# A two-block transformer kernel on one core: the second block run twice on 256 tokens, the first time while expert rows are still gathered

## The chip, the cores and the metric

The kernel runs on one core of a Trainium2 chip. The metric is the time of one execution on the device, in microseconds.

## The reference, cut to what matters

The input is 512 tokens of width 1024. The first block (adaptive norm, windowed attention, a short convolution, and a product-key expert layer) is followed by a second block: a matrix-LSTM layer, cross-attention to 256 memory rows, an MLP of width 4096, then a pooling mixer, cross-attention and an MLP again. All are float32. The part of the expert layer that the change is about, and the parts of the second block that tie tokens together:

```python
        ue = jnp.take(u_tab, idx, axis=0)          # 128 rows of 1024 for each token
        ve = jnp.take(v_tab, idx, axis=0)
        act = gelu(jnp.einsum('thkd,td->thk', ue, t))
        return jnp.einsum('thk,thkd->td', (g * act), ve)
...
def second_block(x, mem, ...):
    for i in range(DEPTH_2):                       # 2 layers
        y = mlstm_mixer(...) if i == 0 else pool_mixer(...)
        x = layer_norm(ALPHA * x + y, ...)
        x = layer_norm(ALPHA * x + memory_cross_attn(...), ...)
        x = layer_norm(ALPHA * x + sq_relu_mlp(...), ...)
```

In the second block a token depends on itself and on earlier tokens only (the LSTM's decay sums, a causal convolution over 4 tokens, means over the last 2 to 16 tokens). So tokens 0 to 255 can pass through all of it without tokens 256 to 511.

## The kernel before, in words

Features lie on partitions, tokens along the free axis. A weight tile (128 outputs x 1024 inputs, 512 KB) is streamed from HBM into a ring of four by SyncE. ScalarE rounds it to `whi` (`upper`), VectorE forms the rest `wlo` (`lower`), and TensorE forms `whi*x`, `whi*xlo`, `wlo*x` for 8 blocks of inputs: 24 matmuls of 512 columns for one tile (`feature_product`). The second block has 195 of the 277 tiles. Products go round four PSUM banks (`RING`); bank 4 to 7 serve sums, scores and transposes. All engines run code in the order in which it is written and meet at semaphores.

The expert layer has 512 *picks*: pick p is one expert row for each of 128 tokens (p // 128 is the group of tokens). GpSimd gathers u and v of a pick together, 128 rows of 8 KB (1.05 MB), into one of 8 slots (`gather`, line 400). VectorE multiplies u by the tokens and adds up (`expert_dot`, line 1743). ScalarE applies GELU, multiplies by the gate, and scales an identity matrix by it (`expert_weight`, lines 1145, 1149, 1154). TensorE multiplies this diagonal by v, two float32 matmuls of 512 columns, into banks 4 and 5 (`expert_sum`, line 676). After each 128 picks the sums are turned and added to `xres` (`turn_peer`, `add_peer`). VectorE chooses experts 32 picks at a time, between dots (`top_keys`, `top_pairs`, `pick_experts`; a *unit*). Between picks 288 and 415, 16 weight tiles of the memory's keys and values are worked on.

Only when pick 511 is added does the second block begin: `norm 3`, the LSTM's 17 input tiles (`lstm`), its heads (`core`, 8 tiles), its output (`lout`, 8), then for each layer cross-attention (`xq`, `xo`, 8 tiles each) and MLP (64 tiles), with the pooling mixer (2 tiles, part of it on GpSimd) between the layers. After every one a layer norm over features needs all eight products, so TensorE waits for a chain over ScalarE and VectorE.

Of the kernel before, what the change touches and what calls it, by code (L numbers as in the profile page):

```python
# [6 lines left out]
ALU = mybir.AluOpType  # L7
ACT = mybir.ActivationFunctionType
AX = mybir.AxisListType
F32 = mybir.dt.float32  # L10
# [19 lines left out]
SLOTS = 8  # L30
# [4 lines left out]
MEM_AT, MEM_EVERY = 288, 8  # L35
FF = 4096
WINDOWS = (2, 4, 8, 16)
MIX_ORDER = (1, 0, 3, 2, 5, 4, 7, 6)
# [16 lines left out]
for _name, _n in (("ident", P), ("ones", P), ("perm", P), ("iota", P), ("utri", P), ("band", 3 * P), ("cos", T),  # L55
                  ("sin", T), ("cnt", 4 * 16)):
    _CONST[_name] = (_at, _n)
    _at += _n
# [3 lines left out]
def plan():  # L62
# [37 lines left out]
    section("lstm", [1] * 17)  # L100
    section("core", [1, 1, -2] * 4)
    section("lout", [1] * 8)
    for layer in range(2):
        if layer:
            section("pool", [4] * 2)
        section(f"xq{layer}", [1] * 4 + ([-2] + [1] * 2) * 2 + [-2, -2])
        section(f"xo{layer}", [1] * 8)
        section(f"mlp{layer}", [1] * 4 + ([1] * 4 + [2] * 4) * 7 + [2] * 4)
# [5 lines left out]

SEMAPHORES = (
    "tile_done", "early_done", "bank_free0", "bank_free1", "bank_free2", "bank_free3", "w_loaded0", "w_loaded1",
    "w_loaded2", "w_loaded3", "w_split", "consts_in", "vecs_in", "ctx_in", "conds_in", "mod_dot", "mod_in0",
    "mod_in1", "mod_in2", "mod_in3", "x_in", "mod_used", "norm_out", "stored", 
# [4 lines left out]
    "diagonal", "pick_used", "peer_summed", "peer_copied", "peer_turned", "experts_in0", "experts_in1", "experts_in2",  # L123
    "experts_in3", "experts_in4", "experts_in5", "experts_in6", "experts_in7", "ident_ready",
    "mem_split", "split3", "rows_ready", "decay_turned", "floor_read", "max_spread", "lstm_weighted",
    "qk_ready", "lstm_scores", "head_rms_read", "decay_copied", "lstm_den", "decay_arg", "floor_spread",
    "head_squares", "head_rms", "lstm_split", "pool_split", "x_scores_read", "x_scores", "x_probs", "x_turned_copied",
    "x_turned", "split4", "split5", "split6", "split7", "split8", "hidden_split", "squared", "inverse_ready",
# [3 lines left out]
    "pool_added", "x_shift", "x_exp", "mlp_start", "ppad_zero", "pool_step", "odd_split", "act_step", "dve_step",  # L132
# [3 lines left out]
def build(nc, a, out):  # L136
    ctx = ExitStack()
    with ctx:
# [31 lines left out]
        slots_all = placed("slots", [P, SLOTS, 2 * D], split_at)  # L170
        identr = placed("identr", [P, P], arena_at + 4 * 8192, F32R)[:, :]
        mem_hi = placed("mem_hi", [P, KB, CT], arena_at, F32R)
        mem_lo = placed("mem_lo", [P, KB, CT], arena_at + 4 * 2048, F32R)
# [48 lines left out]
        cand = flat_acc[:, 1024:1536]  # L222
        look = flat_acc[:, 1536:2048]
        tokens = work[:, :, :].rearrange("p k t -> p (k t)").rearrange("p (t d) -> p t d", t=TT)
        dot_out = ar(12288, 1024)
        diag = flat_acc[:, 512:768].rearrange("p (a n) -> p a n", a=2)

        def peer_tokens(t):
            return tiles_of(8192 if t < 2 else 4096, 2, T)
# [1977 lines left out]
```

## Time and profile before

| | us |
|---|---|
| median of 3 runs | 3341.86 (3335.34 to 3342.62) |
| the profiled execution | 3341.29 |
| its span | 3339.2 |
| mean granted TensorE clock | 0.943 |

The span is the time from the first instruction to the last; the rest of the profiled execution's time, 2.1 us, lies around it. A page of the profile gives for each engine the busy time and its share, then the same in 40 slices of the span. A busy TensorE is not one at its peak: its matmuls overlap in the records, and the distance from one start to the next is what one costs in a row.

### The profile page before, as it was taken

Reading aid. Unit: us, or ns where it says so; the run is one execution under the profiler, and the core shown is the slowest. Engines: PE = TensorE matmul, PEld = TensorE weight load, DVE = VectorE, ACT = ScalarE, POOL = GpSimd, SP = SyncE. Lnnn points to the kernel's source line nnn. Section 1 sums busy time; section 2 is a strip of 40 time slices with the busy share of each in tenths; the row PEclk is TensorE's granted clock in tenths of the full one; section 3 lists DMA queues with packets and bytes.
Section 4 is the critical chain, followed back from the end, with each engine's and each line's share of the span. In section 5 each row is a group of like instructions: output and inputs, shape, how many; then the busy total and the mean of one; then the engine's idle time right before and its main releaser. Section 6 shows DMA issues by size and latency. Waiting matters only on the chain. (4 is left out here: it accounts for less than half of the span.)

```text
span 3339.2 us, 32780 instructions
## 1 busy us (share of the span) xinstructions
PE 2908.7 (87%) x10628; PEld 1918.4 (57%) x10628; DVE 2063.9 (62%) x4038; ACT 1193.9 (36%) x2627; POOL 581.1 (17%) x545
## 2 busy tenths in 40 slices
PE   6999899877778777888878789989899986989998
PEld 6777777523333323444433257767788864778886
DVE  6785454566666667667766463665644467564445
ACT  3346323343333333444433344332322223332222
POOL 0000000344444444443434300000000011000000
PEclk9999799999999998999999989999999987999998
DMA  6531122899999999999999922111222220122221
GB/s 243 194 114 57 42 91 70 320 421 419 419 410 417 419 414 406 421 416 417 410 410 421 422 79 69 45 59 61 76 95 94 94 76 19 57 82 95 91 98 51
DMA packets 126110, 719.24 MB, mean 215 GB/s; under 512 B 13200, under 2 KB 16400, under 8 KB 60176
## 3 DMA queue, kind: packets, MB, share of 16 engines
q0 software_dynamic: 73728, 536.90, 39.0%
q1 hardware_dynamic: 46560, 161.18, 14.4%
q10 hardware_dynamic: 5680, 19.40, 1.6%
q8 instruction: 72, 1.18, 0.1%
q14 instruction: 70, 0.57, 0.0%
HBM read 715.33 MB, written 2.10 MB: 215 GB/s over the span
## 5 line engine op out<-in xcount | busy, mean ns | idle before, releaser
L676 PE MATMUL psum<-slots,acc 128*128 128x512 f32 x2048 | 1007.3, 638 | 256.0 <-ACT acc L1154 255.4
L676 PEld LDWEIGHTS psum<-slots,acc 128*128 128x128 f32 x2048 | 390.8, 201 | 851.6 <-ACT acc L1154 445.5
L1743 DVE SCALAR_TENSOR_TENSOR arena<-slots,work 128x1024 f32<-128x1024 f32 x512 | 627.9, 1226 | 401.3 <-DMA slots<-in_experts,consts 385.2
L400 POOL DMA_INDIRECT slots<-in_experts,consts x512 | 553.4, 1081 | 1362.1 <-PE psum L676 713.6
L431 PE MATMUL psum<-xhi,whi 128*128 128x512 f32 x1104 | 445.7, 404 | 3.7 <-DVE wlo L1376 3.7
L432 PE MATMUL psum<-xlo,whi 128*128 128x512 f32 x1104 | 436.8, 396 | 0.0
L433 PE MATMUL psum<-xhi,wlo 128*128 128x512 f32 x1104 | 436.7, 396 | 0.0
L1376 DVE TENSOR_TENSOR wlo<-w,whi 128x1024 fp32r<-128x1024 f32 x277 | 336.8, 1220 | 153.0 <-ACT whi L954 152.0
L954 ACT ACTIVATE whi<-w 128x1024 fp32r<-128x1024 f32 x277 | 291.1, 1052 | 287.3 <-PE psum L433 287.3
L431 PE MATMUL psum<-yhi,whi 128*128 128x512 f32 (+1 forms) x736 | 296.6, 403 | 34.1 <-POOL ylo L418 21.1
L1145 ACT ACTIVATE consts<-consts 128x1 f32<-128x1 f32 x512 | 101.7, 199 | 574.5 <-DVE arena L1743 573.3
L432 PE MATMUL psum<-ylo,whi 128*128 128x512 f32 (+1 forms) x736 | 293.7, 399 | 0.0
L433 PE MATMUL psum<-yhi,wlo 128*128 128x512 f32 (+1 forms) x736 | 293.5, 399 | 0.0
L1154 ACT ACTIVATE acc<-consts 128x128 f32<-128x128 f32 x512 | 205.5, 401 | 174.4 <-PE psum L676 159.4
L431 PEld LDWEIGHTS psum<-xhi,whi 128*128 128x128 f32 x1104 | 207.8, 188 | 59.1 <-issue 10.6
L433 PEld LDWEIGHTS psum<-xhi,wlo 128*128 128x128 f32 x1104 | 207.5, 188 | 50.7
L432 PEld LDWEIGHTS psum<-xlo,whi 128*128 128x128 f32 x1104 | 207.7, 188 | 49.8 <-issue 1.6
L431 PEld LDWEIGHTS psum<-yhi,whi 128*128 128x128 f32 x736 | 141.4, 192 | 73.5 <-issue 25.5
L432 PEld LDWEIGHTS psum<-ylo,whi 128*128 128x128 f32 x736 | 141.8, 193 | 33.8 <-issue 0.2
L433 PEld LDWEIGHTS psum<-yhi,wlo 128*128 128x128 f32 x736 | 141.4, 192 | 33.7
L1149 ACT ACTIVATE consts<-consts 128x1 f32<-128x1 f32 x512 | 150.8, 295 | 17.6
L2056 DVE TENSOR_TENSOR acc<-acc,psum 128x512 f32<-128x512 f32 x112 | 77.0, 688 | 123.1 <-PE psum L433 123.1
(266 smaller groups left out, 3036.5 us busy)
## 6 DMA issues: line engine op xcount, KB each, us to landing
w<-in_stream SPq DMA_DIRECT2D x277, 512.0 KB, 3.4
arena<-in_wmod SPq DMA_DIRECT2D x4, 2048.0 KB, 17.8
arena<-in_wmod ACTq DMA_DIRECT2D x8, 1024.0 KB, 6.0
acc<-in_wmod ACTq DMA_DIRECT2D x8, 1024.0 KB, 7.9
slots<-in_experts,consts POOLq DMA_INDIRECT x512, 13.3
xres<-in_xT SPq DMA_DIRECT2D x1, 2048.0 KB, 15.2
outT<-xres SPq DMA_DIRECT2D x8, 256.0 KB, 2.0
consts<-in_consts SPq DMA_DIRECT2D x1, 1056.0 KB, 5.0
```

The costliest lines, as they stand in the source:

```text
L400: pool.indirect_dma_start(out=slots[p % SLOTS], out_offset=None, in_=a["experts"], in_offset=bass.IndirectOffsetOnAxis(ap=indices[:, p:p + ...
L431: pe.matmul(dst, hi, xh(k), start=(j == 0), stop=False)
L432: pe.matmul(dst, hi, xl(k), start=False, stop=False)
L433: mm = pe.matmul(dst, lo, xh(k), start=False, stop=(j == len(ks) - 1))
L676: mm = pe.matmul(bank(4 + half), diag[:, p % 2, :], v[:, half * T:(half + 1) * T], start=(c == 0), stop=(c == PICKS - 1))
L954: act.activation(whi[:, s, :, :].rearrange("p k n -> p (k n)"), w32[:, s, :], ACT.Copy)\
L1145: act.activation(gelus[:, c:c + 1], inner[:, c:c + 1], ACT.Gelu).then_inc(sem("gelu_ready"), 1)
L1149: act.activation(weights[:, c:c + 1], gelus[:, c:c + 1], ACT.Copy, scale=gates[:, p:p + 1])\
L1154: act.activation(diag[:, p % 2, :], ident, ACT.Copy, scale=weights[:, c:c + 1])\
L1376: dve.tensor_tensor(wlo[:, s, :, :].rearrange("p k n -> p (k n)"), w32[:, s, :], whi[:, s, :, :].rearrange("p k n -> p (k n)").bitcast(F32 ...
L1743: dve.scalar_tensor_tensor(dot_out, slots[p % SLOTS][:, 0:D], 1.0, tokens[:, p // PICKS, :], ALU.mult, ALU.mult, accum_out=inner[:, c:c + ...
L2056: free(dve.tensor_tensor(acc[:, k, :], acc[:, k, :], bank(oo % RING), ALU.add), oo)
```

## The change

- The whole second block is written as functions of a half (`half_lstm_in`, `half_lstm_core`, `half_cross`, `half_mlp`, `half_pool`), called for tokens 0 to 255 and then for 256 to 511. So its 195 weight tiles are streamed, rounded and split twice (472 tiles in all, 277 before), each with 24 matmuls of 256 columns. In the MLP's second layer two outputs of a tile share one bank of 512.
- Picks 0 to 255 go as before, but into 6 slots at first, which grow to 10 (`SLOT_OPENS`). A unit's choice follows each 21 picks instead of 32 (`TOP_AT`), with 3, 3 and 4 dots between its parts. The memory's tiles come at picks 96 to 223.
- Picks 256 to 511 are spread over the first half's tiles by a table (`pick_ends`): 1 share for a tile, 2.4 for a tile of `core`, 2.5 to 6 for a norm. That is 10 picks ahead of the first tile, 71 over the first MLP's tiles and 71 over the second's. TensorE's part is `sum_picks`, ScalarE's `weigh_picks`, VectorE's `dot_picks`.
- For these picks u and v are gathered apart, 4 KB rows from two tables, v two picks behind u: 4 places for u, 6 and later 8 for v.
- Two of these picks are added at once by eight matmuls with 64 rows and 64 columns of weights and 512 columns of data (`expert_pair`), into four banks: rows 0 to 63 of v into banks 4 and 5, rows 64 to 127 into 6 and 7. The diagonal is 128 x 64.
- In the first half products have two banks instead of four (`out_banks`), sums and norms banks 2 and 3. The loops over the MLP's groups are written out.
- The pooling mixer is on VectorE alone. The first half's outputs are stored from GpSimd's queue.

```diff
-SLOTS = 8
+EARLY = NPICKS // 2
-MEM_AT, MEM_EVERY = 288, 8
+MEM_AT, MEM_EVERY = 96, 8
+H = T // 2
+HT = H // P
...
+    for half in range(2):
+        section(f"lstm{half}", [1] * 17)
+        section(f"core{half}", [-1 - half, 1, 1, -3] * 4)
+        section(f"lout{half}", [1] * 8)
...
+    first, last = SECTIONS["lstm0"][1], SECTIONS["lstm1"][1]
+    banks = [o % (2 if first <= o < last else RING) for o in range(len(DONE))]
...
+    gaps = {SECTIONS["lout0"][0] + 7: 2.5, SECTIONS["pool0"][0] + 1: 2.5, SECTIONS["mlp0"][0] + 63: 6}
...
+    length = {n: 2.4 if n in core else 1.0 for n in range(first, last)}
+    total = sum(length.values()) + sum(gaps.values())
+    head = EARLY + 10
...
+SLOT_OPENS = {60: 7, 84: 6, 144: 8, 228: 9}
...
+U_ROWS, V_ROWS, V_OPEN, LEAD = 4, 6, 300, 2
...
+LATE_UNITS = 12
+TOP_AT = {u: 2 + 21 * (u - 1) if u < LATE_UNITS else EARLY + 1 + 11 * (u - LATE_UNITS) for u in range(1, UNITS)}
...
-            for p in range(NPICKS):
+            for p in range(EARLY):
                 gather(p)
...
+            for p in range(EARLY, NPICKS + LEAD):
+                if p < NPICKS:
+                    gather_u(p)
+                if p >= EARLY + LEAD:
+                    gather_v(p - LEAD)
...
+            def expert_pair(p):
+
+                t, c = p // PICKS, p % PICKS
+                if c == 1:
+                    pe.wait_ge(sem("peer_added"), 8 * t)
+                for q in (p - 1, p):
+                    row, _, uses = V_USE[q - EARLY]
+                    pe.wait_ge(sem(f"v_in{row}"), 16 * uses)
+                pe.wait_ge(sem("diagonal"), p + 1)
+                for half in range(2):
+                    for q in (p - 1, p):
+                        for r in range(2):
+                            rows = slice(64 * r, 64 * r + 64)
+                            to = 64 * (r ^ (q % 2))
+                            mm = pe.matmul(psum[to:to + 64, 4 + 2 * r + half, :], diag(q)[rows, :],
+                                           v_row(q)[rows, half * T:(half + 1) * T], start=(c == 1),
+                                           stop=(c == PICKS - 1))
+                        if half:
+                            mm.then_inc(sem("pick_used"), 1)
...
+            def sum_picks(n):
+
+                nonlocal summed
+                while summed < picks_by(n, True):
+                    expert_sum(summed)
+                    if summed % PICKS == PICKS - 1:
+                        turn_peer(summed // PICKS)
+                    summed += 1
...
+            def half_linear(n, o, XH=XHH, XL=XLH):
+                linear(n, o, XH, XL, H)
+                sum_picks(n)
...
+            for half in range(2):
+                half_lstm_in(half)
+                half_lstm_core(half)
+                half_cross(half, 0)
+                half_mlp(half, 0)
+                half_pool(half)
+                half_cross(half, 1)
+                half_mlp(half, 1)
```

The order in which TensorE goes over the first MLP's tiles shows the first term: these rows are matmuls (line, output, inputs, columns). Before:

```order
L431 MATMUL psum<-yhi,whi 128x512
L432 MATMUL psum<-ylo,whi 128x512
L433 MATMUL psum<-yhi,wlo 128x512
L431 MATMUL psum<-yhi,whi 128x512
L432 MATMUL psum<-ylo,whi 128x512
```

In the changed kernel, the first half, where one tile ends and the next begins:

```order
L604 MATMUL psum<-xhi_h,whi 128x256
L605 MATMUL psum<-xlo_h,whi 128x256
L606 MATMUL psum<-xhi_h,wlo 128x256
L874 MATMUL psum<-arena,consts 64x512 x8
L604 MATMUL psum<-yhi_h,whi 128x256
L605 MATMUL psum<-ylo_h,whi 128x256
L606 MATMUL psum<-yhi_h,wlo 128x256
```

A matmul has half the columns, and between two tiles of every second pick stand the eight of 64 weights' columns.

VectorE in the second layer of the MLP, where a tile's rest (`wlo`) is formed and the hidden values are squared and split. Before:

```order
L2040 TENSOR_TENSOR work<-work 128x512
L1382 CAST yhi<-work 128x512
L1384 TENSOR_TENSOR ylo<-work,yhi 128x512
L1376 TENSOR_TENSOR wlo<-w,whi 128x1024
L2040 TENSOR_TENSOR work<-work 128x512
```

In the changed kernel, the first half, where outputs are collected and the next group's first hidden tile comes (line 2035 is the dot of one pick):

```order
L1656 TENSOR_TENSOR wlo<-w,whi 128x1024
L2035 SCALAR_TENSOR_TENSOR slots,consts<-slots,work 128x1024
L2401 TENSOR_TENSOR acc<-acc,psum 128x512
L1656 TENSOR_TENSOR wlo<-w,whi 128x1024
L2035 SCALAR_TENSOR_TENSOR slots,consts<-slots,work 128x1024
L2401 TENSOR_TENSOR acc<-acc,psum 128x512
L1656 TENSOR_TENSOR wlo<-w,whi 128x1024
L2035 SCALAR_TENSOR_TENSOR slots,consts<-slots,work 128x1024
L2401 TENSOR_TENSOR acc<-acc,psum 128x512
L1656 TENSOR_TENSOR wlo<-w,whi 128x1024
L2035 SCALAR_TENSOR_TENSOR slots,consts<-slots,work 128x1024 x2
L2394 TENSOR_TENSOR work<-work 128x256
```

The rest of a tile has its 1024 columns as before, the hidden values have 256, and about one dot of a pick stands at each tile.

GpSimd's queue of gathers, with what each waits for. Before:

```order
L400 DMA slots<-in_experts,consts 128x2048 x3
L400 DMA slots<-in_experts,consts 128x2048 [waits pick_used] x24
L400 DMA slots<-in_experts,consts 128x2048 [waits pick_used,picked]
L400 DMA slots<-in_experts,consts 128x2048 [waits pick_used] x31
L400 DMA slots<-in_experts,consts 128x2048 [waits pick_used,picked]
```

In the changed kernel, late in the first half:

```order
L578 DMA arena<-in_expert_v,consts 128x1024 [waits pick_used]
L563 DMA slots<-in_expert_u,consts 128x1024 [waits dotted,picked]
L578 DMA slots<-in_expert_v,consts 128x1024 [waits pick_used]
L563 DMA slots<-in_expert_u,consts 128x1024 [waits dotted]
L578 DMA slots<-in_expert_v,consts 128x1024 [waits pick_used]
```

A pick has two gathers of 1024 columns, where u waits for a dot four picks back, and v for a sum.

## Rows read from the trace of the kernel before

**Rows 1.** The page: busy time of the engines, DMA in 40 slices

```profile
PE 2908.7 (87%) x10628; PEld 1918.4 (57%) x10628; DVE 2063.9 (62%) x4038; ACT 1193.9 (36%) x2627; POOL 581.1 (17%) x545
DMA  6531122899999999999999922111222220122221
```

**Rows 2.** By stretch: us, PE, PEld, DVE, ACT, POOL busy, clock, DMA share, GB/s

```profile
617.00:1930.00 1313.00, 1054.58 (x2486) 444.86 (x2484) 891.12 (x2056) 524.96 (x1679) 549.35 (x508) 0.94 1.01 414
1930.00:1968.00 38.00, 25.30 (x94) 18.86 (x95) 24.96 (x50) 17.90 (x29) 0.00 (x0) 0.78 0.00 1
1968.00:2057.00 89.00, 85.40 (x384) 68.77 (x384) 44.23 (x53) 39.24 (x55) 0.00 (x0) 0.99 0.30 100
2057.00:2161.00 104.00, 103.84 (x426) 72.43 (x426) 69.35 (x109) 36.47 (x52) 0.00 (x0) 0.98 0.10 31
2161.00:2206.00 45.00, 43.70 (x200) 35.03 (x198) 27.59 (x39) 13.60 (x18) 0.00 (x0) 1.00 0.29 87
2221.00:2308.00 87.00, 80.34 (x320) 59.51 (x320) 53.98 (x129) 31.91 (x63) 0.00 (x0) 0.96 0.14 44
2308.00:2353.00 45.00, 44.76 (x192) 35.91 (x192) 19.75 (x27) 11.06 (x14) 0.00 (x0) 1.00 0.23 75
2353.00:2367.00 14.00, 6.64 (x35) 5.97 (x34) 10.29 (x19) 4.58 (x6) 0.00 (x0) 0.70 0.26 91
2367.00:2730.00 363.00, 361.12 (x1536) 289.32 (x1536) 196.25 (x260) 99.04 (x116) 0.00 (x0) 0.99 0.28 90
2730.00:2797.00 67.00, 26.29 (x82) 20.58 (x83) 58.56 (x96) 19.50 (x29) 27.41 (x28) 0.63 0.06 21
3317.00:3339.00 22.00, 6.50 (x33) 6.02 (x32) 13.79 (x25) 7.23 (x10) 0.00 (x0) 0.59 0.25 95
```

**Rows 3.** Timeline of GpSimd: the first gathers

```profile
618.55 0.93 POOL L400 DMA_INDIRECT slots<-in_experts,consts  x1 [29.84 <-PE psum L433]
619.78 0.94 POOL L400 DMA_INDIRECT slots<-in_experts,consts  x1 [0.30 <-issue]
```

**Rows 4.** Waits of the whole span: total us, times, longest

```profile
POOL slots L400 <- PE psum L676: 713.6, 414, 8.7
DVE arena L1743 <- DMA slots<-in_experts,consts: 385.2, 312, 2.4
```

**Rows 5.** Timeline of TensorE, 512 and 256 columns, then a run of sums

```profile
2400.14 0.40 PE L431 MATMUL psum<-xhi,whi 128*128 128x512 f32 x1
2400.38 0.39 PE L432 MATMUL psum<-xlo,whi 128*128 128x512 f32 x1
...
1351.66 0.28 PE L433 MATMUL psum<-mem_hi,wlo 128*128 128x256 f32 x1
1351.78 0.28 PE L431 MATMUL psum<-mem_hi,whi 128*128 128x256 f32 x1
...
1439.82 7.21 PE L676 MATMUL psum<-slots,acc 128*128 128x512 f32 x16
```

**Rows 6.** Groups of VectorE by form, 1960 to 3339 us

```profile
L1376 DVE TENSOR_TENSOR wlo<-w,whi 128x1024 fp32r<-128x1024 f32 x191 | 232.1, 1220 | 71.6 <-ACT whi L954 71.5
L2056 DVE TENSOR_TENSOR acc<-acc,psum 128x512 f32<-128x512 f32 x112 | 77.0, 688 | 123.1 <-PE psum L433 123.1
```

**Rows 7.** Groups of VectorE by form, 700 to 1900 us

```profile
L1743 DVE SCALAR_TENSOR_TENSOR arena<-slots,work 128x1024 f32<-128x1024 f32 x467 | 572.8, 1227 | 365.6 <-DMA slots<-in_experts,consts 350.9 <-issue 3.2
L1743 DVE DVE_READ_ACCUMULATOR arena<-slots,work 128x1 f32 x467 | 38.6, 83 | 0.0
L1384 DVE TENSOR_TENSOR mem_lo<-acc,mem_hi 128x256 fp32r<-128x256 f32 x8 | 3.4, 426 | 0.3
L1382 DVE CAST mem_hi<-acc 128x256 fp32r<-128x256 f32 x8 | 2.3, 289 | 0.0
```

**Rows 8.** A group of ScalarE by form, 700 to 1900 us

```profile
L1145 ACT ACT_TABLE_LOAD x14 | 18.0, 1283 | 0.2
```

**Rows 9.** A group of TensorE by form, whole span

```profile
L589 PE MATMUL psum<-arena 128*64 128x128 f32 x288 | 44.2, 306 | 0.7 <-ACT arena L1063 0.7
```

More of the change, by code:

```diff
@@ L99, in plan @@
     section("memv", [1] * 8)
[L100 to L108, printed above, removed]
+    for half in range(2):
+        section(f"lstm{half}", [1] * 17)
+        section(f"core{half}", [-1 - half, 1, 1, -3] * 4)
+        section(f"lout{half}", [1] * 8)
+        for i in (2 * half, 2 * half + 1):
+            if i % 2:
+                section(f"pool{half}", [4] * 2)
+            section(f"xq{i}", [1] * 4 + ([-1] + [1] * 2) * 2 + [-1, -1])
+            section(f"xo{i}", [1] * 8)
+            section(f"mlp{i}", [1] * 64)
@@ new lines, in pick_ends, with by @@
+def pick_ends():
+    first, last = SECTIONS["lstm0"][0], SECTIONS["lstm1"][0]
+    core = range(SECTIONS["core0"][0], SECTIONS["lout0"][0])
+    gaps = {SECTIONS["lout0"][0] + 7: 2.5, SECTIONS["pool0"][0] + 1: 2.5, SECTIONS["mlp0"][0] + 63: 6}
+    groups = [first]
+    for i in range(2):
+        gaps[SECTIONS[f"xo{i}"][0] + 7] = 2.5
+        groups += [SECTIONS[f"xq{i}"][0], SECTIONS[f"mlp{i}"][0]]
+    length = {n: 2.4 if n in core else 1.0 for n in range(first, last)}
+    total = sum(length.values()) + sum(gaps.values())
+    head = EARLY + 10
+    ends, at = {first - 1: (EARLY, head)}, 0.0
+    def by(at):
+        return head + round((NPICKS - head) * at / total)
+    for n in range(first, last):
+        begin = ends[n - 1][1]
+        at += length[n]
+        end = begin if n in groups else by(at)
+        at += gaps.get(n, 0)
+        ends[n] = (end, by(at) if n in gaps else end)
+    assert ends[last - 1][1] == NPICKS
+    return ends
@@ new lines, with picks_by, slot_uses @@
+PICK_ENDS = pick_ends()
+def picks_by(n, gap=False):
+    return PICK_ENDS[n][gap] if n in PICK_ENDS else EARLY if n < SECTIONS["lstm0"][0] else NPICKS
+SLOT_OPENS = {60: 7, 84: 6, 144: 8, 228: 9}
+SLOT_UNITS = {7: 4, 8: 8, 9: 12}
+def slot_uses():
+    free, slots = [4, 5, 0, 1, 2, 3], []
+    for p in range(EARLY):
+        if p in SLOT_OPENS:
+            free.insert(0, SLOT_OPENS[p])
+        slots.append(free.pop(0))
+        free.append(slots[-1])
+    before, uses, last = [], [], {}
+    for p, slot in enumerate(slots):
+        before.append(last.get(slot))
+        uses.append(slots[:p + 1].count(slot))
+        last[slot] = p
+    return slots, before, uses, last
@@ L1337, in _ @@
[L1337 to L1346 removed]
+                n, o = SECTIONS[f"xo{q}"]
```

1697 lines of the change are left out of this document (958 added, 739 removed).

## The prediction

> **What bounds the kernel now.** I read the page first: TensorE is busy 87% of the span, but the DMA line shows two halves that look unlike each other, full for some 16 slices and at one to two tenths after them [rows 1]. So I cut the span into stretches [rows 2]. From 617 to 1930 us the DMA engines are busy throughout at 414 GB/s, while VectorE is busy for 891 of 1313 us and ScalarE for 525. These are picks 4 to 511: 508 gathers and 16 weight tiles of half a gather's size each, so 1313 / 516 = 2.545 us for a gather and 1.27 us for a tile. VectorE waits for rows in 312 places, 385 us in all; GpSimd's wait for TensorE (714 us) is only the wait for a free slot [rows 4]. This stretch is bound by DMA, and TensorE's work in it (two matmuls a pick) is covered. Then the second block starts, and DMA is nearly idle: an MLP takes 363 us with TensorE busy in 361 of them, `lout` 45 us for 8 tiles, and only the norms, the pooling stretch (67 us, TensorE busy 26) and `core` hang on other engines [rows 2]. So the span now is 617 us up to the gathers that flow, 1313 of DMA, and 1409 mostly of TensorE. The change tries to lay half of the first bound beside half of the second.
>
> **Prices.** TensorE: one matmul of 512 columns starts 0.234 us after the one before it, one of 256 after 0.12 (0.118 over the run that these rows are from) [rows 5]. A tile of 24 costs 5.6 us before and 2.83 now: a half costs half, weights loaded twice or not. A float32 matmul of a pick has 7.21 us for 16, which overlap, so about 0.43 each and 0.86 for a pick [rows 5]. VectorE: a tile's rest has 1.22 us and does not shrink; collecting an MLP output of 512 columns 0.69 [rows 6]; 256 columns 0.43, as a cast 0.29; a dot 1.23 + 0.08 = 1.31 [rows 7]. A unit's choice of experts: (891 - 508 x 1.24 - 20 for 16 rests - 14 for splits and sums) / 15 = 15 to 16 us busy, about 18 with the gaps between dependent instructions [rows 2, 7].
>
> **Part 1, up to pick 255.** Before, picks 0 to 3 are gathered while the slots of the rest wait 29.8 us for the projection, to 618.6 [rows 3]. Now only two slots are free of it, so 254 rows come after: 254 x 2.545 + 16 x 1.27 = 667 us. Six slots instead of eight are less cover. A slot's round is 8 x 2.545 = 20.4 us before and 15.3 with six; a landing, dot, diagonal, sum and new gather need some 9 of it (my sum of those rows). A unit's three parts now have 10 dots between start and end: 31 us for which DMA needs 25.5, and with the peaks VectorE falls up to 11 us behind where six slots cover 6. I take 4 to 5 us for each of the three units before pick 60 and 4 for the rest: +18. Part 1 ends at 618.6 + 667 + 18 = 1303.
>
> **Part 2, the first half with 256 picks.** In the MLP a tile has 71/64 = 1.11 picks. DMA: 1.27 + 1.11 x 2.545 = 4.09 us. VectorE: a hidden tile 1.22 + 0.43 + 0.29 + 0.43 = 2.37, an output tile 1.22 + 0.69 = 1.91, so 2.14 + 1.11 x 1.31 + gaps 0.15 = 3.74. TensorE: 2.83 plus the pick. The trace has no concurrent partial-array matmuls; the nearest row is one of 64 weight columns, 306 ns for 128 columns [rows 9], but it stands alone. Bounds: four quadrants side by side, 2 x 0.43 a pair, 0.43 a pick; all eight one after another, 8 x 0.43 / 2 = 1.72. I take 0.75, near the lower end, as quadrants of other rows and other banks share nothing that the code shows. TensorE then needs 3.66. All three lie within 12% of each other and DMA leads: 64 x 4.09 = 262, +6 for imperfect covering and the slow first tiles: 268 a time, instead of 363 for all tokens.
> Two rules bear on this and pull apart. The Trainium skill, "TensorE: Matmul & The Clock Gate" (Part 3: Packing small matmuls), reports 2.4 to 3.1 times from three or four tiles; by that a pick would have 0.55 to 0.72 us. "TensorEngine Tiling (Array Packing)", Key Properties of the Trainium skill, says that a change of tiling mode drains the engine, which happens twice a pair here. No row of this trace shows either.
>
> The other stages are VectorE's, which carries dots, rests and the half's own chains in program order. Its sum for part 2: 256 dots 335 us, 195 rests 238, 4 units 66, the half's own work about 365 (the instructions of one half at 256 columns), together 1004, gaps 60. By stage: 10 picks, a unit and norm 3: 48; `lstm` 118 (norm output 9, convolution 8 x 4.7, 9 tiles x 2.7, gates 12, two units 36; ScalarE reloads a table for each switch between Silu and GELU, 1.28 us [rows 8], hidden here); `core` 112 (four heads of 23 busy and 5 waited; 104 before); `lout` 36; four norms 14 to 15 each, 58, and the one after the pool 12; `xq` 58 twice, `xo` 36 twice (9 picks each and 8 tiles, 33 by DMA); two MLPs 536; the pooling mixer on VectorE with its norm 50 (8 x 4.1 + 17). Sum 48 + 118 + 112 + 36 + 58 + 12 + 116 + 72 + 536 + 50 = 1158. DMA alone would need 256 x 2.545 + 195 x 1.27 = 899, so it is idle a fifth of this part. Part 2 ends at 2461.
>
> **Part 3, the second half, four banks and no picks.** Halved where TensorE bounds, less where a chain does; the times before are those of [rows 2]: MLP 186 twice (363; VectorE's 2.3 a tile hides under 2.83); `lout` 29; `xo` 23 twice; `xq` 45 twice (87 before, VectorE's softmax and rests now last); norm 3: 15; `lstm` 60 (together 127 before, 1930 to 2057); `core` 78 (104; the same instructions, shorter); four norms 12 (14), with that behind the pool 46; the mixer 40 (67); the end 15 (22). Sum 372 + 29 + 46 + 90 + 15 + 60 + 78 + 46 + 40 + 15 = 791, and the end is at 3252. Plus the 2.1 us around the span: **3255 us** against 3341.3 for the profiled execution, which lies 0.6 us under the median. That is 2.6% less. The gain is small for 652 us of gathering (256 x 2.545) laid beside the half: the half beside it grows from about 791 to 1158, and 195 rests, 238 us of VectorE, come twice in chains of small instructions that did not halve.
> Free: the doubled stream (102 MB, 248 us of DMA in part 3 under 791), the store from GpSimd's queue, and 512 gathers instead of 256 (1.24 us from one issue to the next, 618.55 to 619.78 [rows 3], so 2.5 a pick against 4.09 / 1.11 = 3.7). Were GpSimd slower than that, every MLP tile would follow it.
>
> **Rivals.**
> 1. *Quadrants don't overlap (0.12).* A pick then has 1.72 us and the switches; say 1.9. An MLP tile is bound by TensorE at 2.83 + 1.11 x 1.9 = 4.94, 316 us each instead of 268, +96; some 20 in the other stages: **3370**, slower. It decides from 1.14 us a pick on, where 2.83 + 1.11 x 1.14 passes 4.09. For it: all partial-array matmuls of the trace are single. Against: they share no rows, columns or banks.
> 2. *The engines' orders interlock (0.15).* In the first half products have two banks, so product n + 2 waits until ScalarE or VectorE has read n, and these stand behind a dot (1.31), a rest (1.22) or a table load and a pick's three steps. If reading takes more than the 2.83 us of one product, the difference is lost in each tile; 0.7 us in 195 tiles are 137: **3392**, slower. For it: before, with four banks and no picks, ScalarE and VectorE still wait for each product. Against: both have 3 to 10% left in the MLP and reading comes early after a product.
> 3. *Half-size gathers move less (0.04).* If 12 gathers of 0.5 MB in flight don't fill the engines as 8 of 1 MB did, and a pick costs a third more, 3.4 us, an MLP has 64 x 1.27 + 71 x 3.4 = 323, +110 for two: **3365**, slower. Weight tiles have this size, but never come back to back in the trace; against it, both moves have several in flight. The Trainium skill, "DMA: Bandwidth & Descriptors" (Measured, HBM to SBUF), asks for at least 1 MiB a transfer; no row here shows it.
> 4. *Better covering (0.07).* Twelve places let DMA run ahead in slow stages; part 2 is then VectorE's 1060: **3155**.
>
> **Numbers.** My forecast has 0.62, its own range 3170 to 3330. The measurement can tell about 0.2% (7 us) from no change. Faster: nearly all of mine and rival 4, some of the rest: 0.69; within 7 us 0.04; slower: rivals 1 to 3 but for a sixth, 0.27. The range for all goes from 3140 to 3390, which leaves out the ends of rival 2.
>
> **What would show it.** Pick 255's dot near 1300; then DMA at four fifths; first MLP near 268 us at over 0.9 DMA, TensorE's eight matmuls of a pair in under 2 us; the second half's MLP 186 us each; VectorE over 85% in part 2. I would be wrong most in `lstm` and `core` of the first half, where I added waits by judgement, and by the quadrants.

## The result, and the profile after

The change made the kernel slower by 0.8%: 3367.39 us, median of three runs (3363.34 to 3370.86), against 3341.86 (3335.34 to 3342.62), a ratio of 1.0082 with the interval 1.0055 to 1.0108. I had forecast 3255 us. The direction was wrong.

The page of the kernel after, its line for TensorE and its DMA line, answers to [rows 1]:

```profile
PE 2813.9 (84%) x16524; PEld 2123.3 (63%) x16524; DVE 2377.0 (71%) x5028; ACT 1500.2 (45%) x3177; POOL 882.8 (26%) x781
DMA  6531122799999999686679988479993223551353
```

The full slices of DMA are no longer one block. They end after pick 255, come back twice, in the two MLPs of the first half, and in between stand at six to eight tenths or lower. The stretches answer to [rows 2] (us, busy time of PE, PEld, DVE, ACT and POOL, granted clock, DMA share, GB/s). In order: part 1; norm 3, `lstm`, `core` and `lout` of the first half; `xq` and `xo`; its first MLP; pooling; its second MLP; the first MLP of the second half, each with the norm before it:

```profile
617.00:1318.00 701.00, 562.67 (x1446) 254.40 (x1444) 509.30 (x1268) 284.07 (x883) 290.21 (x257) 0.91 0.98 396
1360.00:1627.00 267.00, 204.22 (x1362) 146.21 (x1361) 216.81 (x520) 158.72 (x326) 119.01 (x105) 0.84 0.74 269
1627.00:1744.00 117.00, 95.88 (x643) 73.08 (x640) 78.29 (x165) 61.51 (x131) 43.23 (x40) 0.88 0.71 250
1744.00:2082.00 338.00, 286.51 (x2213) 219.71 (x2209) 241.36 (x409) 152.73 (x361) 182.01 (x157) 0.93 0.90 343
2082.00:2135.00 53.00, 20.44 (x96) 14.08 (x96) 46.40 (x143) 18.93 (x44) 6.54 (x6) 0.56 0.24 86
2248.00:2556.00 308.00, 276.29 (x2159) 216.16 (x2160) 228.28 (x383) 147.34 (x340) 160.57 (x137) 0.94 0.90 347
2833.00:3031.00 198.00, 186.88 (x1554) 186.01 (x1554) 150.39 (x245) 90.39 (x122) 0.00 (x0) 0.97 0.52 173
```

Beside the forecast: `lstm` to `lout` 267 us (266), `xq` and `xo` with a norm 117 (108), pooling 53 (50), the second half's MLP 198 with its norm (186 + 12). The two MLPs with picks carry the miss: 338 and 308 where 283 had been forecast (268 and a norm). In them no engine and not DMA is full over the whole stretch: TensorE 85% and 90%, VectorE 71% and 74%, DMA 90%. So "which one is the bound" has no answer from this table alone, and the experiments had to give it.

### The profile page after: what moved, and what is told of

It reads as the page before. It is cut to its first block and busy times, and to the rows that moved or that the text cites. A ratio compares the mean times of both kernels' runs of the same rounds, so it can differ in the third digit from the quotient of the medians.

```text
span 3365.6 us, 47654 instructions
## 1 busy us (share of the span) xinstructions
PE 2813.9 (84%) x16524; PEld 2123.3 (63%) x16524; DVE 2377.0 (71%) x5028; ACT 1500.2 (45%) x3177; POOL 882.8 (26%) x781
## 5 line engine op out<-in xcount | busy, mean ns | idle before, releaser
L2035 DVE SCALAR_TENSOR_TENSOR slots<-slots,work 128x1024 f32<-128x1024 f32 x453 | 553.6, 1222 | 131.1 <-DMA slots<-in_experts,consts 107.8
L856 PE MATMUL psum<-slots,acc 128*128 128x512 f32 x788 | 406.3, 658 | 120.1 <-ACT acc L1388 113.8
L544 POOL DMA_INDIRECT slots<-in_experts,consts x197 | 219.4, 1114 | 928.7 <-DVE consts L2007 582.7
L563 POOL DMA_INDIRECT slots<-in_expert_u,consts x256 | 285.9, 1117 | 558.8 <-DVE slots L2035 507.2
L604 PE MATMUL psum<-yhi_h,whi 128*128 128x256 f32 x1312 | 381.1, 290 | 55.7 <-ACT acc L1623 25.8
L604 PE MATMUL psum<-xhi_h,whi 128*128 128x256 f32 x1456 | 420.7, 289 | 3.9 <-DVE wlo L1656 3.9
L605 PE MATMUL psum<-xlo_h,whi 128*128 128x256 f32 x1456 | 410.9, 282 | 0.0
L606 PE MATMUL psum<-xhi_h,wlo 128*128 128x256 f32 x1456 | 410.4, 282 | 0.0
L605 PE MATMUL psum<-ylo_h,whi 128*128 128x256 f32 x1312 | 374.9, 286 | 0.0
L606 PE MATMUL psum<-yhi_h,wlo 128*128 128x256 f32 x1312 | 374.1, 285 | 0.0
L874 PE MATMUL psum<-slots,consts 64*64 64x512 f32 x1080 | 237.7, 712 | 137.9 <-ACT consts L1388 87.3
L604 PEld LDWEIGHTS psum<-yhi_h,whi 128*128 128x128 f32 x1312 | 254.8, 194 | 98.5 <-issue 78.2
L604 PEld LDWEIGHTS psum<-xhi_h,whi 128*128 128x128 f32 x1456 | 278.7, 191 | 44.4 <-issue 36.5
L874 PEld LDWEIGHTS psum<-slots,consts 64*64 64x64 f32 x1080 | 61.6, 150 | 233.3 <-issue 221.6
```

Of the source, the lines that this page charges most:

```text
L544: pool.indirect_dma_start(out=slots[slot], out_offset=None, in_=a["experts"], in_offset=bass.IndirectOffsetOnAxis(ap=indices[:, p:p + 1], ...
L563: pool.indirect_dma_start(out=u_rows[row], out_offset=None, in_=a["expert_u"], in_offset=bass.IndirectOffsetOnAxis(ap=indices[:, p:p + 1], ...
L604: pe.matmul(dst, hi, xh(k), start=(j == 0), stop=False)
L605: pe.matmul(dst, hi, xl(k), start=False, stop=False)
L606: mm = pe.matmul(dst, lo, xh(k), start=False, stop=(j == len(ks) - 1))
L856: mm = pe.matmul(bank(6 + half), diag(p), v[:, half * T:(half + 1) * T], start=(c == 0), stop=(c == PICKS - 1))
```

## The experiments

Runs of one kernel scatter: three of the kernel after lie 7.5 us apart, four of e4 19 and six of h1 22. All of e2, e3, f and g ran once, so a difference of less than some 20 us in their whole time says little; there the stretches within the trace carry the reading. All of batch e shared its runs of before (3339.21 us, seven runs), all of batch f one run (3341.08), all of batch g one (3342.16).

**e1: the kernel before with rows gathered apart.** Only the form of the gather changes: two of 4 KB rows for one of 8 KB rows. The products and their order stay.

```
-                pool.indirect_dma_start(
-                    out=slots[p % SLOTS], out_offset=None, in_=a["experts"],
+                for j, table in enumerate(("expert_u", "expert_v")):
+                    pool.indirect_dma_start(
+                        out=slots[p % SLOTS][:, j * D:(j + 1) * D], out_offset=None, in_=a[table],
...
-                dve.wait_ge(sem(f"experts_in{p % SLOTS}"), 16 * (p // SLOTS + 1))
+                dve.wait_ge(sem(f"experts_in{p % SLOTS}"), 32 * (p // SLOTS + 1))
```

> The kernel before, with u and v of each pick gathered by two DMAs of 4 KB rows instead of one of 8 KB; nothing else differs. In the changed kernel DMA moved only 377 GB/s at a full share in the middle of the first MLP, against 414 before. Theory A (4 KB gathers are slower by themselves): the gathering stretch of 1313 us grows by a tenth, to about 1430, and the time to 3450. Theory B (what slows it is the mix with the stream of weight tiles): 3342, unchanged within 10 us. A third way: GpSimd's 1.24 us for each issue, 2.48 a pick against 2.545, becomes the limit and adds up to 60 us.

Measured: 3505.1 us (four runs), ratio 1.049 (1.0473 to 1.0508), 166 us more over 512 picks. The stretches of this kernel inside its gathering:

```profile
617.00:1300.00 683.00, 487.05 (x972) 191.11 (x970) 411.26 (x986) 229.66 (x759) 489.34 (x474) 0.89 0.97 366
1300.00:2100.00 800.00, 607.09 (x1514) 273.90 (x1515) 480.03 (x1070) 282.28 (x917) 569.63 (x542) 0.87 0.97 367
```

The DMA engines are 97% busy (101% before), but move 366 GB/s instead of 414, 11.6% less. So theory A holds, with more than its 3450 us. GpSimd has 489 of 683 us busy, 72%, so it isn't the full one. A gather in two halves costs about 2.545 + 166 / 512 = 2.87 us. The prediction had charged the late picks 2.545. Whether the shorter rows or the smaller gathers cost this isn't separated: both changed.

**e2: a quarter of u.** The late picks' u rows are gathered over 256 of 1024 columns; a late pick moves 640 KB instead of 1 MB, and its dot stays full length. (Besides the line shown, the table holds only these columns, and the dot's factor is 0.1.)

```
-                    out=u_rows[row], out_offset=None, in_=a["expert_u"],
+                    out=u_rows[row][:, 0:256], out_offset=None, in_=a["expert_u"],
```

> The changed kernel, where a gather of u after pick 255 brings 256 of 1024 columns (the dot still runs over 1024, so its result is another). An MLP tile then moves 0.52 + 1.11 x 0.66 = 1.25 MB instead of 1.69. Theory A (DMA sets the pace of the first half's MLPs): both shrink by 20 to 35 us down to VectorE's 3.7 to 3.9 us a tile, and the whole by 60 to 90 us, near 3290. Theory B (the engines' orders set it, DMA is only busy beside them): less than 20 us in all.

Measured: 3348.5 us, 19 less, at the edge of the scatter and of theory B. The MLPs took 322 and 300 us instead of 338 and 308. Three eighths of a late pick's bytes bought 16 of the 55 us by which the first MLP had missed. From 1780 to 1900 us, inside the first MLP, DMA is no longer full and TensorE is:

```profile
1780.00:1900.00 120.00, 118.86 (x988) 93.66 (x987) 99.00 (x159) 62.05 (x146) 76.83 (x66) 1.00 0.89 306
```

DMA sets some of the pace; TensorE stands close behind it.

**e3: no late picks.** Picks 256 to 511 are neither chosen, gathered, dotted nor summed; two halves and two banks stay. Two of its edits:

```
-            for p in range(EARLY, NPICKS + LEAD):
+            for p in range(0):
...
-                while summed < picks_by(n, True):
+                while False:
```

> The changed kernel without the picks 256 to 511: their choice, gathers, dots, diagonals and sums are left out, everything else stands. It gives the price of the first half alone and so what the picks cost in it. Theory A (halving itself costs little, two banks are enough): the first half takes as long as the second, 800 to 815 us, the whole 2940. Theory B (two banks stall the first half): 850 or more, the whole near 3000.

Measured: 2909.2 us, where theory A had 2940. Four stretches of this kernel, `lstm` to `lout` and the two MLPs of the first half (two banks), then the first MLP of the second half (four banks):

```profile
1326.00:1490.00 164.00, 139.10 (x946) 129.26 (x946) 109.07 (x222) 82.37 (x132) 0.00 (x0) 0.87 0.31 100
1575.00:1777.00 202.00, 189.67 (x1554) 188.25 (x1554) 151.48 (x246) 90.87 (x122) 0.00 (x0) 0.96 0.56 170
1906.00:2108.00 202.00, 189.74 (x1554) 188.23 (x1554) 151.43 (x246) 90.95 (x122) 0.00 (x0) 0.96 0.55 170
2378.00:2576.00 198.00, 186.86 (x1553) 186.00 (x1553) 150.48 (x245) 90.50 (x122) 0.00 (x0) 0.97 0.56 173
```

Without picks two banks cost 4 us an MLP against four. So the half itself is sound, and this run gives a ledger. The start of pick 255's dot and the end of the span are in each trace:

```
                              before    after     e3
pick 255's dot (us)           1262.6    1318.1    1314.5
pick 511's dot                1930.4
end of the span               3339.2    3365.6    2907.4

part 1 longer                 1318.1 - 1262.6                    = + 55.5   (forecast + 40)
gathering of 256 picks gone   1930.4 - 1262.6                    = -667.8
halving the second block      (2907.4-1314.5) - (3339.2-1930.4)  = +184.1   (forecast +173)
256 picks beside a half       (3365.6-1318.1) - (2907.4-1314.5)  = +454.6   (forecast +367)
sum                                                              = + 26.4
```

The 667.8 us hold 16 weight tiles of the memory besides (16 x 1.27 = 20 us), which stand in part 1 of the kernel after and so in its + 55.5. A late pick still costs 454.6 / 256 = 1.78 us of the span, against 2.545 in the gathering, and I had forecast 367 / 256 = 1.43. That one line holds 88 of the 114 us by which the span was missed.

**e4: fewer picks in the MLPs.** The table that shares out the picks gives tiles of the MLPs a weight of 0.85 and the other tiles 1.4 (both 1.0 in the change).

```
-    length = {n: 2.4 if n in core else 1.0 for n in range(first, last)}
+    length = {n: 2.4 if n in core else 1.4 for n in range(first, last)}
+    for i in range(2):
+        at = SECTIONS[f"mlp{i}"][0]
+        for n in range(at, at + 64):
+            length[n] = 0.85
```

> The changed kernel with another table: a tile of an MLP has the share 0.85 and every other tile but those of core 1.4, so that each MLP has some 13 picks fewer. Theory A (in the MLPs DMA bounds with 2.8 us a pick, in the other stages VectorE with 1.3 to 2): 26 picks moved save 25 to 40 us, near 3335. Theory B (the engines' orders bound everywhere alike): 3367 within 10 us.

Measured: 3376.95 us (four runs), ratio to before 1.0129 (1.0101 to 1.0156). The MLPs fell to 307 and 278, but `lstm` to `lout` rose from 267 to 308 and the others by 8 to 14 each. That is theory B: a pick costs about as much elsewhere as in an MLP, and taking picks from the tiles of an MLP isn't the cure.

**f1 to f3: one engine at a time.** f1 takes the quadrants away, f2 shortens the dots, f3 the sums.

```
f1   for r in range(2):
+        if 1 < c < PICKS - 1:
+            if r:
+                mm = pe.matmul(psum[0:64, 4 + 2 * (q % 2) + half, :], diag(q),
+                               v_row(q)[:, half * T:(half + 1) * T], start=False, stop=False)
+            continue
f2
-    dve.scalar_tensor_tensor(u, u, 1.0, tokens[:, p // PICKS, :], ALU.mult, ALU.mult,
+    w = D if p < EARLY else 256
+    dve.scalar_tensor_tensor(u[:, 0:w], u[:, 0:w], 1.0, tokens[:, p // PICKS, 0:w], ALU.mult, ALU.mult,
f3   for r in range(2):
+        if half and 1 < c < PICKS - 1:
+            continue
```

> The changed kernel, but of each pair's eight 64x64 products of the late picks four are issued instead, each over all 128 rows into 64 partitions (all but the first and the last pair of a token tile); the sums are not the reference's. A pick then holds TensorE for 4 records of 0.43 = 1.72 us, where the changed kernel's trace has 82.2 us for 78 picks = 1.05 us in the first MLP. If TensorE paces a stage with picks, each of 240 picks costs 0.67 us more: +52 us in the first MLP (338 to 390) and +160 in all, about 3525 us. If VectorE paces, or the covering costs what it costs by the hand-over from engine to engine, it stays within 40 us of the changed kernel: 3370 to 3410. If quadrants brought nothing in the changed kernel, no change.

Measured: 3487.1 us, 120 more than the kernel after; the first MLP 369 instead of 338, the second 342 instead of 308. The first line below is a pair of picks in the first MLP of the kernel after, with the tile's matmul that follows; the last is one of f1 (TensorE's timeline: start, us, name, operands, records):

```profile
1906.26 0.28 PE L606 MATMUL psum<-yhi_h,wlo 128*128 128x256 f32 x1
1906.47 1.95 PE L874 MATMUL psum<-slots,consts 64*64 64x512 f32 x16
1908.35 0.39 PE L604 MATMUL psum<-yhi_h,whi 128*128 128x256 f32 x1
```

```profile
1885.84 3.65 PE L874 MATMUL psum<-arena,consts 128*64 128x512 f32 x8
```

Eight float32 matmuls leave 16 records, two each, in 1.95 us. From the last matmul of a tile to the first of the next 2.09 us pass, 0.12 of it the tile's own, so a pick takes (2.09 - 0.12) / 2 = 0.98 us. f1's four matmuls, 8 records, take 3.65, 1.83 a pick. So the quadrants do overlap and are worth 0.84 us of TensorE a pick. 248 of the late picks have f1's form (all but the first and the last pair of two token tiles; I had counted 240), and 120 / 248 = 0.48 us of each comes through. That lies between the forecasts for "TensorE paces" (3525) and for "it does not" (3370 to 3410). TensorE is busy in 343 of the 369 us of the first MLP: at f1's price it is nearly the whole bound, at 0.98 it is not.

> The changed kernel with the late picks' dots over 256 of the 1024 columns; the dots are not the reference's. By 1.227 us for 1024 columns a dot falls to some 0.4 us, 0.8 less for each of 256 picks. If VectorE paces: MLP 0's stretch 338 to about 275 us and the whole 3367 to about 3200 (0.65 us a pick and more saved). If TensorE paces (tile 2.9 + 1.2 x 1.05): less than 15 us in all. If the two hand each other over through two banks so that their works add in part: between, 30 to 45 us in MLP 0 and 80 to 130 in all.

Measured: 3371.2 us, no change. VectorE falls from 241 to 181 us in the first MLP, and that takes 337 instead of 338. VectorE does not set the pace there.

> The changed kernel with the late picks' products over the first 512 of the 1024 columns alone, but for the first and the last pair of a token tile; the sums are not the reference's. TensorE's share of a pick falls from 1.05 to about 0.55 us. If TensorE paces: -40 us in MLP 0 (338 to 298) and -115 us in all, 3250. If VectorE paces: less than 15 us. If both add in part: 15 to 25 us in MLP 0, 40 to 80 in all.

Measured: 3361.9 us, 6 less, within the scatter. TensorE's work in the first MLP falls from 287 to 267 us, the stretch from 338 to 334. A pair falls from 1.95 to 1.09 us, which is 34 us for 39 pairs; only 20 come through, and the granted clock of the stretch is 0.87 where it was 0.93. Taken alone, TensorE doesn't set the pace either.

**f4, g1 to g3: several at once.** f4 is e2, f2 and f3 together. g1 is f4 with v gathered over 512 columns besides. g2 has g1's gathers with full dots and products. g3 is f2 and f3 together with full gathers. The one new edit, in g1 and g2:

```
-                    out=v_rows[row], out_offset=None, in_=a["expert_v"],
+                    out=v_rows[row][:, 0:T], out_offset=None, in_=a["expert_v"],
```

> The changed kernel with all three together: u gathered and dotted over 256 columns, sums over 512; neither is the reference's. The kernel without late picks took 2909 us. If three resources share the cost of covering, what is left of the 458 us is ScalarE's part and the issues: by ScalarE's 0.3 + waits for a pick, 2990 to 3080 us. If a fourth thing that none of the three touches paces the picks (the chain dot, weight, diagonal, product from engine to engine, or GpSimd's issues at 2 x 1.34 us a pick, 256 x 2.7 = 690 us against 1240 there are), it stays above 3200 us.

> The kernel with all three light, and v gathered over 512 columns besides (its products read the same 512 columns); a late pick now moves 384 KB instead of 1 MB. It was at 3287 with 640 KB a pick. If the DMA engines still were what bounds it there: 3220 to 3260. If VectorE's and TensorE's order around the picks is: within 12 us of 3287. It also shows what the covering costs at the least: the kernel without late picks took 2909 us.

> The changed kernel with u gathered over 256 columns and v over 512 (384 KB a late pick instead of 1 MB), all dots and products issued in full; neither is the reference's. The quarter u alone gave 3348. If three resources stand close to each other at 4.1 to 4.2 us a tile of the MLP, taking more of one brings nothing more: 3335 to 3350, since TensorE's 268 us of 322 and its gaps stay. If the gathers alone paced: 3290 or less.

> The changed kernel with quarter dots and half sums, the gathers in full; neither is the reference's. Each alone brought -4 and +4 us. If the gathers hold the pace by themselves once the engines are lighter (the DMA engines 0.99 busy in the first MLP, 1.0 MB a pick and 0.5 MB a tile at 366 GB/s = 4.9 us for 1.2 picks and a tile): 3345 to 3367. If VectorE and TensorE paced in turns, so that only both together bring something: 3290 or less.

Measured: f4 3287.0, g1 3273.6, g2 3335.6, g3 3352.6 us. g2 and g3 came out inside the forecasts by which several limits stand close together and the gathers hold g3. For f4 my first case (2990 to 3080, all that is left would be ScalarE's) was far off; its other case, above 3200 with something that none of the three touches, came true, and g1 lies near its "within 12 us of 3287". To see why, here are 120 us of steady running in the first MLP, 1780 to 1900 us, in which it is well under way in each. First the kernel after, then g2, then g3 (a stretch each, columns as above):

```profile
1780.00:1900.00 120.00, 111.52 (x916) 86.92 (x914) 96.60 (x154) 58.91 (x140) 76.57 (x64) 0.99 1.02 397
```

```profile
1780.00:1900.00 120.00, 119.87 (x976) 93.21 (x973) 98.41 (x161) 63.13 (x149) 78.31 (x65) 0.98 0.71 232
```

```profile
1780.00:1900.00 120.00, 103.14 (x814) 87.32 (x814) 71.36 (x150) 58.33 (x136) 67.16 (x64) 0.97 1.02 406
```

And TensorE's groups in the same 120 us, of the kernel after and of g2. L604 leaves eight records a tile; L874 leaves 16 for a pair of picks, (128 + 64 + 64) / 8 = 32 picks here:

```profile
L604 PE MATMUL psum<-xhi_h,whi 128*128 128x256 f32 x124 | 35.6, 287 | 0.0
L604 PE MATMUL psum<-yhi_h,whi 128*128 128x256 f32 x96 | 27.5, 287 | 0.0
L874 PE MATMUL psum<-slots,consts 64*64 64x512 f32 x128 | 23.3, 601 | 5.6 <-issue 5.6
L874 PE MATMUL psum<-acc,consts 64*64 64x512 f32 x64 | 15.5, 602 | 0.0
L874 PE MATMUL psum<-arena,consts 64*64 64x512 f32 x64 | 9.2, 694 | 2.9 <-issue 2.9
```

```profile
L604 PE MATMUL psum<-xhi_h,whi 128*128 128x256 f32 x139 | 40.4, 291 | 0.0
L604 PE MATMUL psum<-yhi_h,whi 128*128 128x256 f32 x96 | 27.5, 286 | 0.0
```

The kernel after does (124 + 96) / 8 = 27.5 tiles, 4.36 us each; DMA is full at 397 GB/s, TensorE has 5.6 + 2.9 = 8.5 us of idle time ("issue": the profile names no releaser; in g2, with light rows, TensorE is idle for 0.13 us, so probably a row of v was not there), so a pick holds it (120 - 8.5 - 27.5 x 2.83) / 32 = 1.05 us. In g2, with light gathers, DMA drops to 0.71 and TensorE is busy for 119.87 of 120 us; it does 29.4 tiles, 4.08 us each. So DMA leads, and TensorE stands 0.28 us a tile behind it: taking DMA away altogether gives 6%. In g3 both engines are light and DMA is at 1.02 and 406 GB/s again; 28.6 tiles. That is why f2 brought nothing, f3 little, and e2 some 19 us: each takes from one of two limits that almost coincide, VectorE's being the third (96.6 of 120). But that isn't all. Even g1, with 384 KB a pick, quarter dots and half sums, is just 2% under the kernel before: its first MLP takes 301 us, and TensorE is busy in 260 of them, DMA 67%:

```profile
1719.00:2020.00 301.00, 259.87 (x1915) 212.95 (x1915) 181.01 (x409) 152.05 (x361) 166.85 (x156) 0.90 0.67 214
```

Sixty-two of its tiles take 256 us, 4.1 each, where TensorE's own work at full clock is some 3.45 (2.83, and 35 pairs of 1.09 over 62 tiles; an estimate). No engine nor DMA is full here. What holds it, the chain from dot to sum or GpSimd's issues (f4's other case), no run isolates.

**h1: the adding of a token tile's sums two dots sooner.** The turn of a token tile falls into the first MLP, at pick 384. Stretches of the kernel after around it, then the three operations on its path (timelines of TensorE and ScalarE), then TensorE's waits from 1935 to 1975 us (total us, times, longest):

```profile
1900.00:1935.00 35.00, 34.56 (x284) 28.00 (x280) 26.03 (x41) 16.64 (x39) 19.56 (x17) 0.99 0.98 369
1935.00:1975.00 40.00, 30.09 (x194) 24.22 (x195) 18.08 (x31) 11.27 (x25) 13.41 (x12) 0.79 0.65 231
1975.00:2010.00 35.00, 31.39 (x261) 25.43 (x261) 25.22 (x42) 16.77 (x39) 20.13 (x18) 1.00 1.00 377
```

```profile
1936.91 1.95 PE L874 MATMUL psum<-slots,consts 64*64 64x512 f32 x16 [2.35 <-issue]
1938.94 2.06 ACT L1398 ACTIVATE slots<-psum 128x512 f32<-128x512 f32 x4 [5.75 <-PE psum L874]
1941.06 6.34 PE L894 MATMUL psum<-consts,slots 128*128 128x64 f32 x32 [2.20 <-ACT slots L1398]
```

```profile
PE psum L874 <- DVE xres L2047: 5.8, 1, 5.8
PE psum L874 <- issue: 2.4, 1, 2.4
PE psum L894 <- ACT slots L1398: 2.2, 1, 2.2
```

The last sum of tile 2, ScalarE's copy, 32 records of turning, VectorE's adding and the first sum of tile 3 stand in series, and while they run rows are not freed: DMA drops to 0.65. VectorE adds only behind the fourth dot of the next tile, and TensorE waits 5.8 us for it.

```
-                    if dotted % PICKS == 3:
+                    if dotted % PICKS == 1:
```

> The changed kernel, with the adding of a finished token tile's sums placed two dots sooner in VectorE's order (after the second dot of the next tile instead of the fourth). In the changed kernel TensorE waits 5.8 us for this adding once in the first MLP (and 5 us before the second tile's first sum), while VectorE has been idle 8 us shortly before. If the stall at the turn of a token tile is an order's fault: 5 to 12 us less, 3355 to 3362, ratio to the kernel before 1.004 to 1.006. If VectorE then waits for the turned sums while dots stand behind it and rows stay ungathered, the loss is the same or more: 3365 to 3375. Neither gets below the kernel before.

Measured: 3354.7 us (six runs, 3343.56 to 3365.58), ratio to before 1.0051 (1.0034 to 1.0067), against 1.0082 for the change. The first MLP fell from 338 to 324 us, and the wait for L2047 is gone from it (its TensorE waits from 1900 to 1975 us):

```profile
PE psum L874 <- issue: 2.6, 1, 2.6
PE psum L894 <- ACT slots L1398: 2.2, 1, 2.2
```

Not all 14 us are the edit's. The trace is of the fastest of the six runs, 11 us under their median. From the tile before the turn to four tiles behind it, 36.5 us (1934.5 to 1971.0) became 28.7: 8 us, the wait and a little more. Another 4 of the 14 lie ahead of the turn, where nothing was changed, and the second half, where nothing was changed either, is 8 us shorter. By the medians h1 gains 13 us, and the two intervals against before overlap. It remains slower than the kernel before; no kernel here that computes the whole is faster than that.

## Why the prediction was wrong, point by point

**Right.** The quadrants overlap (rival 1 had 0.12, and it fell: 0.98 us a pick between two tiles and 1.05 on average over 120 us, below the bound of 1.14). Halving costs what I said, 184 against 173. The second half was forecast at 791 and a norm of 14.5 and took 809. DMA leads in an MLP with picks in steady running, TensorE is close behind and VectorE third, in that order; DMA over the whole of part 2 stood at four fifths, as said. VectorE did not: 75% of part 2 instead of over 85%.

**Right by luck.** `lstm` to `lout` took 267 us for 266, but its three parts missed and made up for each other: `lstm` 108 for 118, `core` 104 for 112, `lout` with the picks behind it 55 for 36.

```profile
1360.00:1468.00 108.00, 81.41 (x575) 60.91 (x574) 93.53 (x251) 72.12 (x141) 42.76 (x37) 0.85 0.70 252
1468.00:1572.00 104.00, 80.31 (x487) 55.35 (x487) 85.02 (x201) 61.96 (x130) 47.57 (x43) 0.84 0.76 270
1572.00:1627.00 55.00, 42.50 (x301) 29.96 (x301) 38.27 (x70) 24.64 (x58) 28.68 (x26) 0.82 0.80 298
```

**Rival 2**, the interlock of products and readers, did not happen in the MLP, and it is the trace of the kernel after that shows it: of TensorE's 51 idle us in the first MLP only the norm's 4.7 stand before products of tiles. The rest, but for 0.6 in the norm, is before picks' sums and the turn, above all these two:

```profile
PE psum L874 <- issue: 23.8, 10, 3.4
PE psum L874 <- ACT consts L1388: 14.5, 3, 6.9
```

e3 (two banks cost 4 us an MLP) would not have settled it alone, since it has no picks for readers to stand behind.

**The step that failed: "64 x 4.09 = 262, +6 for imperfect covering and the slow first tiles: 268 a time".** It is most of the miss in 256 picks beside a half, 455 us where I had 367. The term took the greatest of three sums for the whole MLP and put at nothing what stands at its ends and at the turn of a token tile. Here is the first MLP of the kernel after in five stretches (norm and two tiles; tiles; the turn; tiles; from the last tile's end to the next norm), and the 62 tiles of the second:

```profile
1744.00:1770.00 26.00, 14.77 (x85) 10.63 (x81) 20.48 (x51) 15.14 (x34) 4.35 (x3) 0.76 0.38 138
1770.00:1934.50 164.50, 156.02 (x1272) 123.43 (x1272) 126.95 (x204) 79.18 (x186) 101.58 (x85) 0.99 1.00 386
1934.50:1971.00 36.50, 26.16 (x164) 21.59 (x163) 14.65 (x26) 9.12 (x20) 11.42 (x10) 0.77 0.66 240
1971.00:2057.00 86.00, 78.07 (x633) 60.72 (x632) 65.03 (x107) 40.51 (x95) 47.32 (x42) 0.98 0.97 363
2057.00:2082.00 25.00, 11.49 (x67) 3.33 (x66) 14.24 (x25) 8.78 (x26) 17.33 (x18) 0.80 0.94 348
```

```profile
2273.00:2543.00 270.00, 252.36 (x2036) 198.06 (x2032) 205.37 (x327) 125.93 (x296) 153.97 (x131) 0.97 0.97 375
```

```
over the forecast, us              first MLP    second MLP
norm and two tiles (22.7)            + 3          + 3      25.8 and 25.5
62 tiles (62 x 4.09 + 6 = 259.6)     + 10         + 10     269.5 in the second, 4.35 a tile
turn of a token tile (0)             + 18         + 13     287.3 - 269.5; the second's turn: 13.4 behind its last tile
picks behind the last tile (0)       + 25           0      24.7
sum                                  + 56         + 26     measured 338 and 308.5 against 282.5
```

- *Seven picks behind the last tile.* 78 dots fall into the first MLP's stretch. 71 belong to its tiles, as I took from the table; the other 7 are the 6 shares that the same table gives to the norm behind the MLP, and no stage of my sum had time for them. TensorE ends the last tile at 2057.2, waits 6.9 us for a diagonal, and the four pairs end at 2082.0. Nothing covers them. In e3, without picks, this place takes 6 us in both MLPs, so 6 of the 25 and of the second's 13 would stand there anyway. The variants e2, f1 to f4 and g1 to g3 leave it at 18 to 27.

```profile
2064.10 1.12 PE L874 MATMUL psum<-slots,consts 64*64 64x512 f32 x2 [6.89 <-ACT consts L1388]
```

- *The turns.* I had no term for them. At pick 384 sum, copy, turn, add and sum stand in series, with DMA at 0.66; at pick 511 the last sum, copy and turn stand between the last tile and the norm. h1 gets about 8 of the first 18 us back by one position in one order.
- *The price of rows gathered apart.* A tile in steady running takes 4.35 us (4.36 from 1780 to 1900), where 1.27 + 70 / 62 x 2.545 makes 4.14. DMA is at 0.97 to 1.00 there, but moves 375 and 386 GB/s instead of 414 (363 in the shorter stretch behind the turn). No trace of before has such a row; I gave it to rival 3, with 0.04 and a third more a pick. It is an eighth more where gathers stand alone (e1) and less beside weight tiles, and came true as a part of the answer, not as a case of its own. The rule beside that rival, at least 1 MiB a transfer (the Trainium skill, "DMA: Bandwidth & Descriptors", Measured, HBM to SBUF), has the right sign: 366 against 414 GB/s for gathers of half the size.
- *TensorE's price of a pick.* I read "7.21 us x16" as 16 matmuls [rows 5]. They are 8, two records each: the page of before has 2048 records for 512 picks of two matmuls.

```profile
L676 PE MATMUL psum<-slots,acc 128*128 128x512 f32 x2048 | 1007.3, 638 | 256.0 <-ACT acc L1154 255.4
```

So a pick before holds TensorE 1.8 us and not 0.86, and my lower bound of 0.43 for the quadrants should have been 0.86. It measured 0.98 to 1.05, not 0.75, so TensorE's tile is 4.08 instead of 3.66. Of itself that stays under DMA's 4.35, and it cost little: f3's TensorE needs some 3.45 us a tile and its two MLPs are 4 us shorter each. The rule that I had weighed (the Trainium skill, "TensorE: Matmul & The Clock Gate", Part 3: Packing small matmuls) reports 2.4 to 3.1 times from three or four tiles. With 7.3 us for eight such matmuls one after another, an estimate at f1's 0.91 us each, the 1.95 us of a pair would be 3.7 times; no run issues them so.

The first two are places where the cover ends, and hold 56 of the 82 us by which both MLPs missed. That is what a sum of maxima leaves out. That they are costs of place follows from the traces and, for one turn, from h1; no run moved the seven picks.

**Part 1**: 15 us later than 1303. The first 128 dots take 355 us against 318 before (5 of the difference are four weight tiles that stand there now), with DMA's share 0.96 against 1.01 up to 980 us. So six slots instead of eight probably cost more than the 18 us that I allowed; other slots there were not tried.

**Open.** Of the 455 us that the picks cost, the MLPs hold 137 + 107 (338 and 308 against 201 each in e3), and `lstm` to `lout` 103 (267 against 164). In the last TensorE waits for diagonals in many short pieces. From 1318 to 2082 us of the kernel after, of which the first MLP has 14.5:

```profile
PE psum L874 <- ACT consts L1388: 69.3, 20, 6.9
```

Which of dot, GELU, weight and diagonal is late in each was not taken apart; e4 shows only that moving picks there costs more than it saves. What holds g1 is open too.

## What to carry to other kernels

Before work is laid beside other work, subtract: what does the covered pick still cost, what does splitting the cover cost? Here 668 us came off, 184 went for halving and 455 for picks that were thought hidden. Then walk along the cover and ask at each end and each turn what stands beside the covered work there: the steady pace was 6% above the greatest of my sums (4.35 against 4.09), the ends and turns were 56 of 82 us. A row of a table that gives work to a gap needs a term in the sum. To find the bound of such a stretch take from one resource alone, then from two: a single one that brings nothing proves only that another is full. And count the records of one known instruction before a price is read from a group.

## What the runs showed of the hardware that I had not expected

Gathers of 128 rows of 4 KB moved 366 GB/s with the DMA engines 97% busy, those of 8 KB 414 (e1 and [rows 2]). A float32 matmul leaves two records in the trace: 8 matmuls on quadrants are x16 in 1.95 us, and 1024 of a whole kernel x2048. Switching from 128x128 weights to 64x64 quadrants and back costs little: 0.21 us from the start of the last matmul of a tile to that of the first of a pair (0.12 within a tile), and 1.88 from there to the next tile's matmul, where the work itself is 1.72 to 1.83, an estimate from 16 x 0.43 / 4 and from half of f1's 3.65. That a change of tiling mode drains the engine (the Trainium skill, "TensorEngine Tiling (Array Packing)", Key Properties) is at most these 0.09 + 0.16 us.
